# Gating the expert rows as they leave PSUM and adding them into a copy of the token rows by accumulating scatters

## What is computed

```
eid  = group * 8 + top-2 expert of that group          # 2 of 32 experts for each of 1152 tokens
gate = softmax(top-2 logits) * p_group[g]
# each expert's tokens in blocks of 128; free slots have gate 0
h   = silu(xb @ w_g[e]) * (xb @ w_u[e])                # (128, 512)
y   = (h @ w_d[e]) * gate[:, None]                     # (128, 1024)
out = zeros.at[tokens].add(y)                          # two expert rows per token
x   = layer_norm(alpha * x + out, ln3_g, ln3_b)
```

## Time and profile before

| | us |
|---|---|
| median of 3 runs (lowest, highest) | 1651.27 (1648.36, 1653.23) |
| span of the profiled execution, first to last instruction | 1645.9 |
| PE busy in the span | 1568.5 (95%) |
| DVE busy | 1017.5 (62%) |
| ACT busy | 783.7 (48%) |
| POOL busy | 259.3 (16%) |
| last scatter issued | 1590.97 |
| first load of expert rows issued | 1597.38 |
| last DVE instruction ends | 1642.67 |

### The profile page before, as it was taken

How to read it: one execution, slowest core, us unless ns; L and a number is a source line. 1 busy time by engine, 2 the same in 40 slices (tenths; PEclk the granted TensorE clock), 3 DMA queues, 4 the chain that set the end, 5 groups by cost and what they waited for, 6 DMA issues and landing times.

```text
span 1645.9 us, 21330 instructions
## 1 busy us (share of the span) xinstructions
PE 1568.5 (95%) x8466; PEld 1315.0 (80%) x8466; DVE 1017.5 (62%) x1335; ACT 783.7 (48%) x1105; POOL 259.3 (16%) x219
## 2 busy tenths in 40 slices
PE   7999999899998999999999988999999999999956
PEld 6877887788876888999878767888888888888842
DVE  5611111677755556222544548989989999999936
ACT  5411021544445012222422223878888888888834
POOL 0000000300035561000122211111011111111005
PEclk9999999999999999999999987999999999999987
DMA  9721111700022645100345545999999999999876
GB/s 353 255 75 39 41 56 59 251 20 21 2 89 62 229 156 200 59 26 14 128 150 177 160 166 190 374 377 389 389 396 393 394 401 396 394 399 383 327 272 285
DMA packets 85989, 351.70 MB, mean 214 GB/s; under 512 B 23411, under 2 KB 28147, under 8 KB 64133
## 3 DMA queue, kind: packets, MB, share of 16 engines
q1 hardware_dynamic: 75764, 330.43, 53.2%
q0 software_dynamic: 9216, 18.89, 3.0%
q10 hardware_dynamic: 912, 1.05, 0.3%
HBM read 321.93 MB, written 43.15 MB: 222 GB/s over the span
## 4 chain that ended last, share of the span: by engine, by line
PE 90%; DVE 3%; ACT 3%; DMA 2%; issue 1%; POOL 0%; DVEq 0%; SPq 0%; POOLq 0%; ACTq 0%
PE M L1299 26%; PE M L1016 11%; PE T L819 6%; PE M L792 6%; PE T L1299 5%; PE M L896 4%; PE T L731 4%; PE T L1360 2%; PE M L731 2%; PE T L1090 2%; PE T L1088 2%; PE T L1089 2%; PE M L1122 2%; PE M L1104 2%; PE T L1418 2%; PE M L1229 1%
## 5 line engine op out<-in xcount | busy, mean ns | idle before, releaser
L1841 DVE TENSOR_TENSOR rounded<-beside,rounded 128x1024 fp32r<-128x1024 f32 (+1 forms) x397 | 472.6, 1234 | 53.5 <-ACT rounded L1728 43.5
L1299 PE MATMUL M<-rounded 128*128 128x512 f32 x1908 | 461.2, 392 | 2.7 <-ACT rounded L1763 1.9
L1299 PEld LDWEIGHTS M<-rounded 128*128 128x128 f32 x1908 | 355.8, 188 | 77.4 <-ACT rounded L1763 2.1
L1728 ACT CAST rounded<-beside 128x1024 fp32r<-128x1024 f32 x256 | 260.5, 1049 | 69.7 <-DMA beside<-in_w_exp_up 58.5
L1016 PE MATMUL M<-rounded 128*128 128x512 f32 x816 | 196.6, 395 | 2.9 <-ACT rounded L1598 1.6
L1016 PEld LDWEIGHTS M<-rounded 128*128 128x128 f32 x816 | 150.1, 188 | 33.7 <-issue 2.0
L1738 ACT CAST rounded<-beside 128x1024 fp32r<-128x1024 f32 x128 | 127.8, 1050 | 26.8 <-DMA beside<-in_w_exp_down 18.4
L1841 DVE TENSOR_TENSOR rounded<-T,rounded 128x512 fp32r<-128x512 f32 (+2 forms) x98 | 92.6, 948 | 34.2 <-ACT rounded L1611 17.6
L1299 PE MATMUL T<-rounded 128*128 128x512 f32 x384 | 108.7, 398 | 0.0
L2500 POOL DMA_INDIRECT expert_rows<-beside,route_out x32 | 36.6, 1144 | 380.5 <-ACT beside L1769 365.2
L731 PE MATMUL T<-tables,arena 128*128 128x128 f32 x548 | 77.1, 285 | 15.1 <-DMA arena<-in_mem_prompt 6.9
(11 more groups left out here) (362 smaller groups left out, 2430.0 us busy)
## 6 DMA issues: line engine op xcount, KB each, us to landing
beside<-in_w_exp_gate SPq DMA_DIRECT2D x64, 1024.0 KB, 8.0
beside<-in_w_exp_up SPq DMA_DIRECT2D x64, 1024.0 KB, 10.9
beside<-in_w_exp_down SPq DMA_DIRECT2D x32, 2048.0 KB, 11.4
arena<-x_rows SPq DMA_DIRECT2D x27, 512.0 KB, 3.7
x_rows<-arena SPq DMA_DIRECT2D x18, 512.0 KB, 3.1
arena<-expert_rows SPq DMA_DIRECT2D x9, 1024.0 KB, 12.7
arena<-in_x_prompt SPq DMA_DIRECT2D x16, 512.0 KB, 4.0
arena<-in_cache_mem_k SPq DMA_DIRECT2D x8, 1024.0 KB, 5.5
```

The source lines that it names most:

```text
L1299: got = nc.tensor.matmul(out, x[xs], (high, low)[ws](w)[:, c:c + 512], start=(first and n == 0), stop=(last and n == 2))
L1728: nc.scalar.copy(as_both(high(c)), both_raw(c)).then_inc(gu_high, 1)
L1841: return nc.vector.tensor_tensor(out, x, highs.bitcast(f32), ALU.subtract)
```

## The change

The gates move into the expert loop, and the sum of the two expert rows and x2 moves into the scatters.

- `store_x2` writes each tile twice, to `x_rows` and to a new DRAM tensor `x2_plus_experts`, which has one tile more than there are tokens: rows for unused slots. Later loads of the x1 tile and the first gathers wait for both.
- DVE works out the gates (divided by alpha) and the selections weighted with them before it goes on with the chunks 4 to 7 of expert 0. PE makes 12 of the unread matmuls and then 18 of 32 columns, which bring the gates to slots (`slot_gate`, one column for each expert).
- `results` multiplies by that column on the way out of PSUM.
- The scatter adds to the rows it writes. All 128 rows of a block are written: unused slots add zero to the spare tile. POOL issues a scatter only when the one before it has landed, because two blocks may add to the same row.
- The last stage loads nine tiles of 512 KB of finished sums, and no x2 and no expert rows. PE has no part in it. The means and variances of tiles 2, 3, 5 and 6 are made by ACT, those of the others by DVE (bn_stats). The order of the steps on DVE, ACT and POOL is written anew.

```diff
-    slot = 2 * (128 * np.arange(9)[None, :, None] + p[:, None, None]) + np.arange(2)[None, None, :] + 1
+    slot = np.stack([128 * np.arange(9)[None, :] + p[:, None] + 1, np.broadcast_to(9 * 128 + 1 + p[:, None], (128, 9))], -1)
...
-    ye_dram = nc.dram_tensor("expert_rows", [2 * NT * P, D], f32).ap()
-    ye_pairs = ye_dram.rearrange("(r k) d -> r k d", k=2)
+    sum_dram = nc.dram_tensor("x2_plus_experts", [(NT + 1) * P, D], f32).ap()
...
+        slot_gate = b_router[:, 0:NE + 1]
...
             def store_x2(t):
                 sp.wait_ge(norm_ready, NT + t + 1)
                 sp.dma_start(x2_dram[t * P:(t + 1) * P, :], xr2[t % 2]).then_inc(norm_out[t % 2], 16)
+                sp.dma_start(sum_dram[t * P:(t + 1) * P, :], xr2[t % 2]).then_inc(norm_out[t % 2], 16)
...
-            for t in range(NT):
-                sp.dma_start(xl[t], x2_dram[t * P:(t + 1) * P, :]).then_inc(ln_in, 16)
             sp.dma_start(gain3, A["ln3_g"].to_broadcast([P, D])).then_inc(ln_in, 16)
             sp.dma_start(shift3, A["ln3_b"].to_broadcast([P, D])).then_inc(ln_in, 16)
             sp.wait_ge(ye_out[1], 16 * (NE // 2))
             sp.wait_ge(ye_out[0], 16 * more + 16 * (NE // 2))
             for t in range(NT):
-                sp.dma_start(yk[t], ye_pairs[t * P:(t + 1) * P, :, :]).then_inc(last_in[t], 16)
-            for n, t in enumerate(SEQ):
-                sp.wait_ge(y_ready, n + 1)
+                sp.dma_start(xl[t], sum_dram[t * P:(t + 1) * P, :]).then_inc(last_in[t], 16)
...
-            for _ in range(20):
+            for _ in range(12):
                 nc.tensor.matmul(M[0][:, 0:512], sel_slot[:, 0, 0, :], sel_slot[:, 0, 0:4, :], start=True, stop=True)
+            pe.wait_ge(sel_ready, 3)
+            for k in (0, 1):
+                for t in range(NT):
+                    to_slots = sel_slot[:, k, t, :] if t < PT else sel_last[:, k, 0, :]
+                    got = nc.tensor.matmul(T[1][:, 0:NE], to_slots.bitcast(f32), r_hot[:, k, t, :], start=(k == 0 and t == 0), stop=(k == 1 and t == PT))
+            got.then_inc(rank_ps, 1)
...
-            pe.wait_ge(wukT_ready, 2)
-            for n, t in enumerate(BY_PE):
-                pe.wait_ge(last_in[t], 32 if t < 4 else 16)
-                if n > 1:
-                    pe.wait_ge(sum_done, NORMS + SEQ.index(BY_PE[n - 2]) + 1)
-                out = T[n % 2]
-                for k in (0, 1):
-                    for c in (0, 512):
-                        got = nc.tensor.matmul(out[:, c:c + 512], diag[2 * n + k], yk[t][:, k, c:c + 512], start=(k == 0), stop=(k == 1))
-                got.then_inc(picks_ps, 1)
...
-                nc.scalar.copy(yo[u], M[1][:, :]).then_inc(ye_rows, 1)
+                nc.scalar.mul(yo[u], M[1][:, :], gate).then_inc(ye_rows, 1)
...
+            def variance(t):
+                n = BY_ACT.index(t)
+                act.wait_ge(last_in[t], 32 if t < 4 else 16)
+                nc.scalar.activation(spread[n], xl[t], ACT.Identity, scale=-1.0 / (32 * D), accum_out=negmean[t]).then_inc(gates_ready, 1)
+                act.wait_ge(gates_ready, NT + 2 + n + 1)
+                nc.scalar.activation(squares[n], xl[t], ACT.Square, scale=1.0 / 32.0, bias=negmean[t], accum_out=varsum[t]).then_inc(var_ready, 1)
+
+            def normalise(t):
+                act.wait_ge(norm_ready, NORMS + t + 1)
+                nc.scalar.activation(xl[t], xl[t], ACT.Identity, scale=rdev[t], bias=shiftof[t]).then_inc(normed3, 1)
+
+            normalise(0)
+            variance(2)
+            normalise(1)
+            variance(3)
+            normalise(2)
+            variance(5)
+            normalise(3)
+            variance(6)
+            for t in (4, 5, 6):
+                normalise(t)
...
             dve.wait_ge(map_ps, 1)
             then(nc.vector.tensor_scalar(r_map, M[1][:, 0:NE], 0.0, 8192.0, ALU.is_equal, ALU.mult))
-            then(nc.vector.scalar_tensor_tensor(route_out[:, 0:NE], M[1][:, 0:NE], -1.0, r_map, ALU.add, ALU.add))
-            nc.vector.tensor_single_scalar(route_tok[:, 0:NE], route_out[:, 0:NE], 1, ALU.logical_shift_right).then_inc(routes_ready, 1)
+            nc.vector.scalar_tensor_tensor(route_tok[:, 0:NE], M[1][:, 0:NE], -1.0, r_map, ALU.add, ALU.add).then_inc(routes_ready, 1)
+            then(nc.vector.tensor_scalar(r_spare, M[1][:, 0:NE], 0.0, spare_id[:, 0:1], ALU.is_equal, ALU.mult))
+            nc.vector.scalar_tensor_tensor(route_out[:, 0:NE], M[1][:, 0:NE], -1.0, r_spare, ALU.add, ALU.add)
+
+            dve.wait_ge(softmax_exp, 4)
+            then(nc.vector.tensor_reduce(r_sum, r_eg, AX.X, ALU.add))
+            then(nc.vector.scalar_tensor_tensor(r_den, r_e2, 1.0, r_sum, ALU.add, ALU.mult))
+            then(nc.vector.tensor_scalar(r_den, r_den, ALPHA, None, ALU.mult))
+            then(nc.vector.reciprocal(gates[:, 0, :], r_den))
+            then(nc.vector.tensor_tensor(gates[:, 1, :], gates[:, 0, :], r_e2, ALU.mult))
+            for k in (0, 1):
+                got = nc.vector.tensor_tensor(r_hot[:, k, :, :], r_hot[:, k, :, :], gates[:, k, :].unsqueeze(2).to_broadcast([P, NT, NE]), ALU.mult)
+            got.then_inc(sel_ready, 1)
...
             gathered_low(0, 0)
+            dve.wait_ge(rank_ps, 4)
+            nc.vector.tensor_copy(slot_gate[:, 0:NE], T[1][:, 0:NE])
...
-                if t in BY_PE:
-                    dve.wait_ge(picks_ps, BY_PE.index(t) + 1)
-                    nc.vector.scalar_tensor_tensor(xl[t], xl[t], 1.0, T[BY_PE.index(t) % 2][:, :], ALU.mult, ALU.add,
-                                                   accum_out=moments[u][:, 0:1]).then_inc(sum_done, 1)
...
+                    nc.vector.bn_stats(tile_stats[t][:, 0:6], xl[t][:, 0:512])
+                    then(nc.vector.bn_stats(tile_stats[t][:, 6:12], xl[t][:, 512:]))
+                    then(nc.vector.bn_aggr(mean_var[t], tile_stats[t]))
+                    nc.vector.tensor_scalar(var_eps[t], mean_var[t][:, 1:2], 1.0, LN_EPS / ALPHA ** 2, ALU.mult, ALU.add).then_inc(softmax_in, 1)
...
+            deviation3(0)
+            deviation3(1)
+            shift_of(0)
+            deviation3(2)
+            shift_of(1)
+            dve.wait_ge(gates_ready, NT + 2)
+            shift_of(2)
+            deviation3(3)
+            deviation3(4)
+            shift_of(3)
+            shift_of(4)
+            add_shift(0)
+            deviation3(5)
+            shift_of(5)
+            add_shift(1)
+            deviation3(6)
+            shift_of(6)
+            add_shift(2)
+            deviation3(7)
+            centre_gain(7)
+            add_shift(3)
+            deviation3(8)
+            centre_gain(8)
             dve.wait_ge(dve_step, step.value())
-            add_shift(PT - 3)
-            add_shift(PT - 2)
-            scale_shift(PT - 1)
-            scale_shift(PT)
+            for t in (4, 5, 6):
+                add_shift(t)
+            scale_shift(7)
+            scale_shift(8)
...
-                nc.gpsimd.indirect_dma_start(out=ye_dram, out_offset=bass.IndirectOffsetOnAxis(ap=route_out[:, column:column + 1], axis=0),
-                                             in_=yo[u], in_offset=None, bounds_check=2 * NT * P - 1,
-                                             oob_is_err=False).then_inc(ye_out[u], 16)
+                nc.gpsimd.indirect_dma_start(out=sum_dram, out_offset=bass.IndirectOffsetOnAxis(ap=route_out[:, column:column + 1], axis=0),
+                                             in_=yo[u], in_offset=None, bounds_check=(NT + 1) * P - 1,
+                                             oob_is_err=True, compute_op=ALU.add).then_inc(ye_out[u], 16)
...
+                if b > 2:
+                    pool.wait_ge(ye_out[1 - b % 2], 16 * ((b - 3) // 2 + 1))
                 if b > 1:
                     scatter(b - 2, b - 2, b % 2)
             for b in (NE - 2, NE - 1):
+                pool.wait_ge(ye_out[1 - b % 2], 16 * ((b - 1) // 2 + 1))
                 scatter(b, b, b % 2)
...
+            for t in (0, 1, 2):
+                inverse_deviation(t)
+            for t in range(7):
+                if t + 3 < NT:
+                    inverse_deviation(t + 3)
+                times_gain(t)
```

More of the change, by code:

```diff
@@ L331, in encoder_layer_kernel @@
         gain3, shift3 = area(WA + 9 * D, D), area(WA + 10 * D, D)
[L332 to L336, removed]
+        centred = [area(WA + (11 + i) * D, D) for i in (0, 1)]
+        spread, squares = ([area(WA + (13 + 2 * i + j) * D, D) for i in range(4)] for j in (0, 1))
+        BY_ACT, WHOLE = (2, 3, 5, 6), (7, 8)
+        BY_DVE = tuple(t for t in range(NT) if t not in BY_ACT)
+        of_tile = [logits[:, t, :] for t in range(NT)]
+        negmean, var_eps, rdev, shiftof = ([s[:, i:i + 1] for s in of_tile] for i in range(4))
+        tile_stats, mean_var = [s[:, 4:16] for s in of_tile], [s[:, 16:18] for s in of_tile]
+        varsum = [s[:, 18:19] for s in of_tile]
         T = [ctx.enter_context(nc.psum_tensor(f"T{u}", [P, 1024], f32)) for u in (0, 1)]
@@ L1397, in _ @@
```

(28 more changed lines are left out.)

130 lines of the change are left out of this document (39 added, 91 removed).

## The result

The changed kernel takes 1678.8 us (1673.5 to 1680.8), the kernel before on the same chip 1649.8 us: a ratio of 1.0182, with a 95% interval of 1.0165 to 1.0200. The forecast was +50 us and it is +29.

The account below looks back on a forecast made before the run. PE and the DMAs were both taken as full, the DMAs with 0.23 us of room a block. Loop +52, last scatter +1.9, last stage -3.7 gave +50: 1702 us from 1651.3, range 1680 to 1725 (whole range 1656 to 1785).

Parts of the forecast that it names:

- Both full, 0.23 us of room: Expert loop: PE and DMAs both full; DMAs' pace 17.54 us a block against PE's 17.77, leaving 0.23.
- p: Expert loop: price of the adding scatter in DMA time, 1.93 us a block, bounds 0.59 and 4.62.
- the sign given: Expert loop, what would show the forecast right: PE idle about 1.7 us a block, waiting for DVE's splits.
- The delay x: Lateness of the last down load, issued at 1566.90 before: 0.3 + 29 p, 56 us.
- The start: Start of the loop: gate steps on DVE ahead of expert 0's splits delay it by 2.1 us, 6 at most.
- The end of the loop: After the last down load, 15 of 24 matmuls follow the last split; loop ends x - 4 later, +52 us.
- The last scatter: Final scatter after the loop: 256 row times instead of 72, 1.9 us longer than 6.30.
- The last stage: Final stage on finished sums: 3.7 us shorter, 41.6 instead of 45.3, with POOL late next.
- Room after all (1): Expert loop: DMAs can reach 426 GB/s, so PE's pace holds; about 1651 us, not slower; chance 0.13.
- Only the rows (2): Expert loop: only the 56 extra rows cost, the add is free, p near 0.59; 1661 us; chance 0.14.
- The chain (3): Expert loop: each scatter's wait for the previous landing sets the pace, 21 to 22 us; about 1762; chance 0.21 with dearer adds.
- rival 2: Expert loop: only the rows count, p near 0.59; 1661 us, range 1656 to 1680; chance 0.14.

Follow-up runs that it names:

- s1: Changed kernel with only used slots added and slots renumbered so a block's rows spread over all 16 DMA engines: 1646.1 us, 1.0000 of the kernel before.
- e1: Changed kernel whose scatters write their 128 rows without adding, so the output lacks the sums: 1643.6 us, 0.998 of the kernel before.
- e3: Changed kernel with odd experts' scatters into a second tensor, left out of the sum, none waiting for the one before: 1676.9 us, 1.0172 of the kernel before.
- e2: Changed kernel with unused slots skipped as out of bounds, 72 adding rows a block on average instead of 128: 1684.8 us, 1.0218 of the kernel before.
- s3: Kernel before, plain rows, with only the slots renumbered over the DMA engines: 1646.5 us, 1.0001 of the kernel before.
- s4: Changed kernel, all 128 rows still added, with slots renumbered so that the gather alone is spread: 1660.7 us, 1.0082 of the kernel before.

## Why the forecast was half right

- **Both full, 0.23 us of room: right.** With p = 1.12 PE waited in most blocks, and where the excess was taken away (s1) PE's pace was back from 1161 us on. The 17.54 held in e1 without the add (17.55). But the sign given was about 1.7 us of idle PE a block, and the trace shows 0.43 (7.6 us in 17.9 blocks), where the pace is 0.89 over PE's own; the rest doesn't stand as idle time in PE's rows.
- **p, the term that was mis-sized:** 1.93 forecast, 1.12 measured, (1.93 - 1.12) x 29 = 23 of the 24 us by which the profiled sum (1696, measured 1671.7) was off; the errors below nearly cancel, which is luck. The price of a row was right: q0's share was forecast near 18% and is 18.7%, so an adding row costs about twice a plain one. That agrees with the two reads and one write that the Trainium skill ("Collectives: The Full Stack", Stop 4) gives for such an add. The step that failed is "(72 + 256 - 144) x 10.5 ns", which spreads all rows evenly over 16 engines and takes the mean for the pace. By the theory of the busiest engine, the 56 rows more fell on the half that had room (e1: no cost), and the add cost the other half 8 row times of 0.168, 1.34 us at most, of which 1.12 showed.
- **The delay x:** 0.3 + 29 x 1.12 = 32.8; measured 29.9 (1596.84 for 1566.90). The first three blocks, up to 1094.05, paid nothing yet. The start, +2.1 forecast, is +1.9.
- **The end of the loop:** x - 4 forecast, x + 0.2 measured. I let 9 of 24 products run ahead of the last split. But `hidden_high` stands behind four casts on ACT and `hidden_low` behind three splits on DVE, so all 24 start at 1611.32; and after 4.97 us of idle time they take 8.30 us for 5.74, with a granted clock of 0.70 from 1612 to 1620.
- **The last scatter:** +1.9 forecast, -0.1 measured. Alone, 128 adding rows take no longer than 72 plain ones.
- **The last stage:** -3.7 forecast, -5.3 measured. POOL's gains start 15.5 us after SP's issue, forecast 15.4, and run back to back but for two waits; they end 1.5 us earlier than forecast, since five roots follow the first gain and not six, and POOL waits 0.76 + 1.27 = 2.0 us for DVE's last tiles and not 2.5. Of the 5.3, 1.0 is lost again between DVE's end and the end of the span.
- **Rivals.** Room after all (1): falls, PE starves. Only the rows (2): falls the other way round, the rows cost nothing and the add everything; its 1661 was off by 18 us on one side, the forecast's 1702 by 23 on the other. The chain (3): falls in e3.
- The measured 1678.8 lies in the whole range, but just below the forecast's own 1680 to 1725, in the stretch given to rival 2 (1656 to 1680, chance 0.14). The number falls there and the mechanism doesn't: the rows alone cost nothing.

## What to carry to other kernels

A DMA share near 1.00 is a mean over 16 engines. Before paying for a new transfer out of it, ask which partitions its rows lie in. By the theory above, which fits the paces measured here, an indirect transfer with skipped rows loads the engines unevenly, and the pace goes by the busiest. Give consecutive used rows to partitions of different engines: here that was one table of numbers and took back the whole 2.2% between e2 and s1. An adding row took 327 ns of an engine for a plain row's 159. Skipping the unused rows of the scatter alone (e2) did not help, since it left the busiest engine as it was.

## What was not expected of the hardware

- 56 more plain rows of 4 KB a block raised the scatters' share from 9.2 to 12.0% and no pace at all (17.54 and 17.55 us).
- A gather of the same 72 rows lands in 8.9 us in s3 and 9.1 in s1 with spread slots, in 10.0 before, in 14.5 and 14.6 beside adding scatters (the changed kernel and e2, median of 32 each), and in 13.8 in s4, where the gather is spread and the scatters still add 128 rows. So spreading the gather alone takes little off its landing.
- A last scatter of 128 adding rows took 6.21 us, one of 72 plain rows 6.30.
